# Experts of a two-layer kernel: first products from split weights, one token tile per group with weights at fixed addresses, further tiles by index

## What is computed

```python
N_GROUPS = 8; EXPERTS_PER_GROUP = 4; EXPERT_FF = 256; D_MODEL = 1024; SEQ = 512

def hierarchical_moe(h, w_router_group, b_router_group, w_router_expert, b_router_expert, w_gate, w_up, w_down):
    group_logits = jnp.matmul(h, w_router_group) + b_router_group
    g_sel = jnp.argmax(group_logits, axis=-1)
    ...
    combine = ...      # (512, 32): two non-zero weights in each token's row
    for e in range(32):
        hid = jax.nn.silu(jnp.matmul(h, w_gate[e])) * jnp.matmul(h, w_up[e])
        out = out + jnp.matmul(hid, w_down[e]) * combine[:, e:e + 1]
```

## Time and profile before

| | us |
|---|---|
| median of 3 runs | 3456.98 (3442.0 to 3465.07) |
| the profiled execution's own time | 3469.57 |
| its span, first to last instruction | 3467.7 |
| PE busy in the span | 3066.9 (88%) |
| DVE busy | 1723.3 (50%) |
| ACT busy | 1076.1 (31%) |
| mean DMA rate | 180 GB/s |

### The profile page before, as it was taken

One profiled execution on the slowest core, in us unless ns is written; L12 is line 12 of the kernel. 1 busy time (PEld: TensorE's weight loads), 2 busy tenths in 40 slices (PEclk: granted clock), 3 DMA queues, 4 the chain that ended last, 5 costly groups with the idle time before them and its releaser, 6 DMA issues. The chain is left out here.

```text
span 3467.7 us, 33649 instructions
## 1 busy us (share of the span) xinstructions
PE 3066.9 (88%) x12681; PEld 2229.5 (64%) x12681; DVE 1723.3 (50%) x3505; ACT 1076.1 (31%) x1596; POOL 488.8 (14%) x357
## 2 busy tenths in 40 slices
PE   7887999699999598778979879698898986999998
PEld 3445666444444244564746568698898986888887
DVE  2255422200000205543442328787879797788886
ACT  2133421100000126674421222234434443333332
POOL 0000000111111000000000000003314143344442
PEclk9995999699999798889779989899999998999999
DMA  3110061488888210021002211357859688999996
GB/s 142 44 50 25 1 145 64 194 329 309 313 315 309 85 49 37 25 97 44 1 26 102 83 55 61 123 193 246 324 178 336 233 305 292 342 369 374 368 374 238
DMA packets 159776, 624.04 MB, mean 180 GB/s; under 512 B 12161, under 2 KB 84481, under 8 KB 128257
## 3 DMA queue, kind: packets, MB, share of 16 engines
q1 hardware_dynamic: 90496, 319.87, 26.1%
q0 software_dynamic: 50688, 276.85, 21.1%
q10 hardware_dynamic: 18432, 25.17, 2.0%
HBM read 555.76 MB, written 66.09 MB: 179 GB/s over the span
## 5 line engine op out<-in xcount | busy, mean ns | idle before, releaser
L1841 POOL DMA_INDIRECT RG<-in_un,EI x128 | 181.6, 1419 | 1400.0 <-DVE EI L2060 1105.3
L2275 PE MATMUL bank<-VH,GL 128*128 128x512 f32 x768 | 300.2, 391 | 29.9 <-DVE VR0r L2264 29.9
L2277 PE MATMUL bank<-VH,GH 128*128 128x512 f32 x768 | 299.7, 390 | 0.0
L1841 POOL DMA_INDIRECT RG<-in_vn,EI x128 | 216.5, 1691 | 446.7 <-DVE X L1855 429.9
L1133 PE MATMUL bank<-UP,HX 128*128 128x512 f32 x480 | 213.0, 597 | 9.4 <-DVE HX L1087 5.5
L1194 DVE SCALAR_TENSOR_TENSOR HN<-SLU,HR,bank 128x256 f32<-128x256 f32 x44 | 21.1, 481 | 344.2 <-ACT SLU L1168 344.2
L2275 PEld LDWEIGHTS bank<-VH,GL 128*128 128x128 f32 x768 | 144.8, 189 | 60.7 <-issue 30.4
L1855 DVE SCALAR_TENSOR_TENSOR X<-RG,DG,X 128x1024 f32<-128x1024 f32 x128 | 164.1, 1282 | 28.2 <-DMA RG<-in_vn,EI 24.1
L1825 PE MATMUL bank<-HTl,UH1r 128*128 128x384 f32 x512 | 174.5, 341 | 0.0
L1826 PE MATMUL bank<-HTh,UH1r 128*128 128x384 f32 x512 | 174.2, 340 | 0.0
L1825 PE MATMUL bank<-HTl,UH0r 128*128 128x384 f32 x512 | 173.3, 338 | 0.0
(11 more groups left out here) (518 smaller groups left out, 6569.3 us busy)
## 6 DMA issues: line engine op xcount, KB each, us to landing
UR<-in_u SPq DMA_DIRECT2D x64, 1024.0 KB, 5.5
VR<-in_vn SPq DMA_DIRECT2D x32, 2048.0 KB, 9.2
W<-in_weights SPq DMA_DIRECT2D x20, 1536.0 KB, 7.3
W<-in_weights SPq DMA_DIRECT2D x14, 2048.0 KB, 8.2
aspill<-GA ACTq DMA_DIRECT2D x128, 192.0 KB, 2.0
wspill<-VR SPq DMA_DIRECT2D x12, 2048.0 KB, 9.2
WW<-wspill SPq DMA_DIRECT2D x32, 768.0 KB, 13.9
AV<-aspill SPq DMA_DIRECT2D x32, 768.0 KB, 16.0
```

The costliest lines, as they stand in the source:

```text
L1841: e.indirect_dma_start(RG[q % RR], None, d["un" if what == "u" else "vn"][:, :], off).then_inc(*row_in[q % RR].up(16))
L2275: e.matmul(bk, r(gl[:, a, t]), r(vh[:, a, :]), start=g == 0 and a == 0, stop=False)
L2277: i = e.matmul(bk, r(gh[:, a, t]), r(vh[:, a, :]), start=False, stop=g == 31 and a == 3)
```

## The change

- The gain goes into `XN` by DVE, 4 multiplies of 128 x 1024 with a row `GR` that SP loads, and no longer into `HX`.
- Slots: tile g (0 to 7) always belongs to group g. Only tokens past the 128th of a group go to tiles 8 to 10, which are given out by count. `IX` holds rows for these 12 units alone; for a tile that no group needs they lie past the end of the weights, and the gather is told to leave out such rows (`bounds_check`, `oob_is_err=False`).
- Units 0 to 31 have weights at fixed addresses. SP loads them: `UP` 0 and 1, and after the logits `DN` 0 to 2 and `UP` 2, in the routing block; the others in the experts block. POOL gathers those of units 32 to 43.
- `UP` is now `W2[n % 3][0]`, and `DN` has three buffers in place of four (two in HT's space).
- The first products become three fp32r passes. ACT makes `UPh` (2 copies of 128 x 2048 a unit) and DVE `UPl` (2 subtractions) one unit ahead, ACT makes `HXh` and DVE `HXl` for the tile. PE waits for each half of `UPl`.
- Weight tiles 21 to 23 are loaded at the end of SP's list in the experts block, and no longer in the routing block.

```diff
@@ routing block @@
-                        load_weights(e, 24)
+                        e.dma_start(GR, d["grow"][1]).then_inc(*gr_in.up(16))
+                        load_up(e, 0)
+                        load_up(e, 1)
+                        e.wait_ge(*e_logit(1))
+                        for n in range(3):
+                            load_dn(e, n)
+                        load_up(e, 2)
...
+                        e.wait_ge(*gr_in(16))
+                        for tb in range(4):
+                            e.tensor_tensor(XN[:, tb, 0:1024], XN[:, tb, 0:1024], GR, ALU.mult).then_inc(*e_gain.up(1))
...
-                        then(e.tensor_scalar(T9, T8, 128.0, None, ALU.mult))
-                        then(e.tensor_tensor(RK[:, 0:4, :], RK[:, 0:4, :], T9.unsqueeze(1).to_broadcast([128, 4, 8]), ALU.add))
+                        then(e.tensor_tensor(T8, T8, cc("iota")[:, 0:8], ALU.subtract))
+                        then(e.tensor_scalar(T9, T8, 128.0, 896.0, ALU.mult, ALU.add))
                         then(e.tensor_tensor(RK[:, 0:4, :], RK[:, 0:4, :], GO, ALU.mult))
-                        then(e.tensor_reduce(SF, RK[:, 0:4, :], AX.X, ALU.add))
+                        vs(e.tensor_reduce(SF, RK[:, 0:4, :], AX.X, ALU.add))
+                        then(e.tensor_tensor(S2, GO, bc(T9), ALU.mult))
+                        vs(e.tensor_reduce(MK, S2, AX.X, ALU.add))
+                        then(e.tensor_scalar(T8, cc("iota")[:, 0:8], 128.0, None, ALU.mult))
+                        then(e.tensor_tensor(S2, GO, bc(T8), ALU.mult))
+                        vs(e.tensor_reduce(s1[:, 0, :], S2, AX.X, ALU.add))
+                        then(e.tensor_scalar(s1[:, 1, :], SF, 127.5, None, ALU.is_gt))
+                        then(e.tensor_tensor(MK, MK, s1[:, 1, :], ALU.mult))
+                        then(e.tensor_tensor(SF, SF, s1[:, 0, :], ALU.add))
+                        then(e.tensor_tensor(SF, SF, MK, ALU.add))
@@ experts block @@
+            def act_tile(e, j, part):
+                e.wait_ge(*m_hturn(2 * j + part + 1))
...
+                e.activation(r(HXh[j % 2][:, span(part, 4), :]), bank[3].rearrange("p (a b) -> p a b", a=4), ACT.Copy).then_inc(*m_hxh.up(1))
+            def act_up(e, n):
+                wait_unit(e, n, up_in, up_in2)
+                if n >= 2:
+                    e.wait_ge(*m_up(n - 1))
+                for s in (span(0, 2048), span(1, 2048)):
+                    e.activation(r(UPh[n % 2][:, s]), UP[n % 3][:, s], ACT.Copy).then_inc(*m_uph.up(1))
+            def dve_up(e, n):
+                for q in range(2):
+                    s = span(q, 2048)
+                    e.wait_ge(*m_uph(2 * n + q + 1))
+                    e.tensor_tensor(r(UPl[n % 3][:, s]), UP[n % 3][:, s], UPh[n % 2][:, s], ALU.subtract).then_inc(*m_upl.up(1))
@@ POOL @@
-                    for n in range(NU):
...
+                    for n in range(4 * NG, NU):
+                        off = bass.IndirectOffsetOnAxis(ap=IX[:, n - 4 * NG:n - 4 * NG + 1], axis=0)
+                        e.wait_ge(*m_up(n - 2))
+                        e.indirect_dma_start(UP[n % 3], None, d["wup"][:, :], off, bounds_check=last, oob_is_err=False).then_inc(*up_in2[n % 3].up(16))
+                        e.wait_ge(*m_down(n - 2))
...
@@ SP @@
+                    for j in range(2):
+                        e.dma_start(HR[j], HS[span(j), :]).then_inc(*hr_in[j].up(16))
+                    for n in range(NU + 3):
+                        if 3 <= n < 4 * NG:
+                            e.wait_ge(*m_up(n - 2))
+                            load_up(e, n)
+                            e.wait_ge(*m_down(n - 2))
+                            load_dn(e, n)
+                        j, x = divmod(n, 4)
+                        if x == 0 and 2 <= j + 1 < NT and n:
+                            e.wait_ge(*m_hn(4 * j))
+                            e.dma_start(HR[(j + 1) % 2], HS[span(j + 1), :]).then_inc(*hr_in[(j + 1) % 2].up(16))
+                        if x == 2 and j >= 1:
+                            e.wait_ge(*m_outA(j))
+                            e.wait_ge(*m_outV(j))
+                            e.dma_start(OS[span(j - 1), :], OT[(j - 1) % 2]).then_inc(*os_done[(j - 1) % 2].up(16))
+                    load_weights(e, 24)
@@ PE @@
-                            for k in range(8):
-                                i = e.matmul(bank[n % 2], HX[j % 2][:, k, :], UP[n % 3][:, span(k, 512)], start=k == 0, stop=k == 7)
+                            for k in range(8):
+                                if k % 4 == 0:
+                                    e.wait_ge(*m_upl(2 * n + k // 4 + 1))
+                                s = span(k, 512)
+                                e.matmul(bank[n % 2], r(xl[:, k, :]), r(UPh[n % 2][:, s]), start=k == 0, stop=False)
+                                e.matmul(bank[n % 2], r(xh[:, k, :]), r(UPl[n % 3][:, s]), start=False, stop=False)
+                                i = e.matmul(bank[n % 2], r(xh[:, k, :]), r(UPh[n % 2][:, s]), start=False, stop=k == 7)
@@ ACT; DVE has dve_up and dve_tile at the same places @@
+                    act_up(e, 0)
+                    act_tile(e, 0, 0)
+                    act_tile(e, 0, 1)
                     for step in range(NU + 2):
                         n = step
+                        if n + 1 < NU:
+                            act_up(e, n + 1)
...
+                        j, x = divmod(step, 4)
+                        if x >= 2 and j + 1 < NT:
+                            act_tile(e, j + 1, x - 2)
```

More of the change, by code:

```diff
@@ L932, in program, with load_up, load_dn, wait_unit @@
             SL_ = sb("slot", [128, 4], c0, I32)
-            IX = sb("IX", [128, NU], c0, I32)
+            IX = sb("IX", [128, NU - 4 * NG], c0, I32)
             scattered = sem("scattered", True)
+            UP, UPl = [a for a, _ in W2], [a for _, a in W2]
+            DN = [HT.rearrange("p k n -> p (k n)")[:, span(n, 2048)] for n in range(2)] + [sb("DN2", [128, 2048], c0)]
+            up_in, dn_in = [sem(f"up_in{n}") for n in range(3)], [sem(f"dn_in{n}") for n in range(3)]
+            up_in2, dn_in2 = [sem(f"up_more{n}", True) for n in range(3)], [sem(f"dn_more{n}", True) for n in range(3)]
+            def load_up(e, n):
+                e.dma_start(UP[n % 3], d["wup"][span(n), :]).then_inc(*up_in[n % 3].up(16))
+            def load_dn(e, n):
+                e.dma_start(DN[n % 3], d["wdn"][span(n), :]).then_inc(*dn_in[n % 3].up(16))
+            def wait_unit(e, n, static, more):
+                if n < 4 * NG:
+                    e.wait_ge(*static[n % 3](16 * (n // 3) + 16))
+                else:
+                    before = len([m for m in range(4 * NG, n) if m % 3 == n % 3])
+                    e.wait_ge(*more[n % 3](16 * before + 16))
             with ExitStack() as c1:
@@ L1029, in _ @@
                         vs(e.tensor_reduce(XN[:, :, 1024:1028], oh.rearrange("p t (g x) -> p t x g", g=8), AX.X, ALU.add))
+                        bc = lambda a: a.unsqueeze(1).to_broadcast([128, 4, 8])
                         e.wait_ge(*e_count(1))
                         then(e.tensor_copy(RK, bank[1][:, 0:40].rearrange("p (b g) -> p b g", b=5)))
-                        then(e.tensor_scalar(TL, RK[:, 4, :], 0.0, None, ALU.is_gt))
-                        for j in range(1, 4):
+                        then(e.tensor_scalar(TL, RK[:, 4, :], 128.0, None, ALU.is_gt))
+                        for j in range(2, 4):
                             then(e.tensor_scalar(T8, RK[:, 4, :], 128.0 * j, None, ALU.is_gt))
@@ L1047, in _ @@
                         then(e.tensor_reduce(GI, GT, AX.X, ALU.add))
-                        then(e.tensor_scalar(GI, GI, 7.0, 512.0, ALU.min, ALU.mult))
-                        then(e.tensor_tensor(IF, cc("rows").unsqueeze(1).to_broadcast([128, NT, 4]), col(GI).to_broadcast([128, NT, 4]), ALU.add))
+                        then(e.tensor_scalar(GI, GI, 512.0, None, ALU.mult))
+                        then(e.tensor_tensor(IF, cc("rows").unsqueeze(1).to_broadcast([128, 3, 4]), col(GI).to_broadcast([128, 3, 4]), ALU.add))
@@ L1057, in _ @@
                             e.indirect_dma_start(HS[:, :], bass.IndirectOffsetOnAxis(ap=SL_[:, tb:tb + 1], axis=0), XN[:, tb, :], None).then_inc(*scattered.up(16))
-            UP = [sb(f"UP{n}", [128, 4096], c0) for n in range(2)] + [HT.rearrange("p k n -> p (k n)")]
-            DN = [sb(f"DN{n}", [128, 2048], c0) for n in range(4)]
+            UPh = [sb(f"UPh{n}", [128, 4096], c0) for n in range(2)]
             HR = [sb(f"HR{n}", [128, 1028], c0) for n in range(2)]
-            HX = [sb(f"HX{n}", [128, 8, 128], c0) for n in range(2)]
+            HXh, HXl = ([sb(f"{x}{n}", [128, 8, 128], c0) for n in range(2)] for x in ("HXh", "HXl"))
             SLU, HN = ([sb(f"{x}{n}", [128, 256], c0) for n in range(2)] for x in ("SLU", "HN"))
@@ L1065, in program @@
             OT = [sb(f"OT{n}", [128, 1024], c0) for n in range(2)]
[L1066 to L1068 removed]
```

(15 more changed lines are left out.)

43 lines of the change are left out of this document (16 added, 27 removed).

## The result

The changed kernel takes 3541.55 us (median of 4 runs, 3534.76 to 3558.93) beside 3461.03 before (median of 4 as well); the ratio is 1.0238, interval 1.0166 to 1.031: slower, 10.5 us over the forecast and inside its range. The profiled execution took 3539.16, its span is 3537.4, 69.7 more than before.

A forecast was written before the change was run, and what follows sets the result against it. PE bounds the stage before; after the change, late-issued UP loads and their landing would. Stage 47, clock 20, start 2 and end 5 sum to +74 on 3469.57: 3543.6, or 3531 as median; range 3483 to 3578.

The forecast's parts named there:

- The step of PE, 9.24 us: Experts stage: PE's work per unit falls from 10.52 to 9.24 us with three fp32r passes, 1.28 less.
- A tile before, 43.0: Experts stage of the kernel before: four steps of 10.52 us plus the tile's own transposes, 43.0 us.
- When SP asks for weights: SP's list in experts: UP n+1 stands behind DN n's wait, leaving one step (9.24 us) of lead; 14.0 needed, plus 0.3.
- The four steps, 51.8 us a tile: Experts, tiles with SP-loaded weights: steps of 11.3, 13.8, 10.1 and 16.6 us, 51.8 a tile, 8.8 more than before.
- Steps 32 to 45, -16: End of experts, where SP loads no weights: left-out gathers cost near nothing, 9.24 a step and 1.6 a tile, -16 us.
- Rival 3: Gathers in experts: rows left out cost as much as rows moved, +40 us over the forecast, 3571; chance 0.08.
- Clock, +20: Experts: PE's eight rests of 7 us lower its clock, 2.5 us each, +20 in all, bounds 0 and +35.
- Start: Routing and first unit: multiplies by GR hidden, slot chain +1.4 us, first unit and tile halves about +0.5.
- Tail, +5: End of experts: loads of weight tiles 21 to 23 meet the gather of rows, which takes twice its 5 us, +5.
- 1: Experts: PE stays the bound and loads are hidden, -42 us, 3415; chance 0.04.
- 2: Experts: landing is the limit, but mildly, within 1%: about +36 us, 3493, or 3483; chance 0.11.
- 4: Experts: the clock stays down through the stage, +150 us over the forecast, 3680; chance 0.03.

The follow-up runs named there:

- tail alone: Changed kernel with SP waiting for the gathers of result rows before loading weight tiles 21 to 23: 3544.3 us, ratio 1.0252 to before.
- order and tail: Changed kernel with each UP and POOL gather asked for once its buffer is free, weight tiles 21 to 23 loaded after the result-row gather: 3404.6 us, 0.9838 to before.

## Why the prediction was right, step by step

- *The step of PE, 9.24 us:* right, 9.2 in the kernels with early loads. *A tile before, 43.0:* 44.0 between `HH` copies. The first step of a tile is 12.0, with 0.8 us in which PE waits for `HX`, and that wait was not in the 43.0; the 473.3 us that seemed to agree end before the last steps' second products.
- *When SP asks for weights:* right, and the one that carries the result. The order alone is worth 119 us of S.
- *The four steps, 51.8 us a tile:* 55.1 measured with the clock's part, forecast 54.3 (51.8 + 2.5). By the means of tiles 2 to 7 the x = 2 step was 0.7 shorter, x = 1 and x = 3 longer by 1.6 and 2.4, where the low clock falls.
- *Steps 32 to 45, -16:* mis-sized. I took a left-out gather at near nothing. It moves nothing, but it has an issue of 1 to 3 us on POOL and 2.1 to landing, with 4.3 of splits behind, and two of them follow the end of a step. The tiles took 42.3, and 39.2 without the gathers: about 9 us more than forecast. Rival 3 (40 more) did not come.
- *Clock, +20:* about 15, by the scaled estimate above. I had counted eight rests of 7 us; the rests at x = 1 lowered the clock too, so there were 17 falls. At x = 3 a step takes 1.9 to 2.7 us more than its rest and 9.6, close to the 2.5 that I took. At x = 1 the slow products take as much again (1.8 to 2.7), and yet the total is not twice as large: that they lie in time without weights anyway is my reading, which no run tests alone.
- *Start:* the multiplies by `GR` were hidden (4.62 us, and DVE still waited 5.6 for the logits). From the logits to the slots it took 12.2 us where it was 11.15: +1.1, forecast +1.4. R fell by 2.2 all the same, with the clock at 0.60 in it and not 0.55; in the three runs with the same routing that reached it at 623 us, as before did, R was 50.5 to 51.0 and not 47.4, so the fall belongs to the execution.
- *Tail, +5:* mis-sized, +10, and 12 for the gather itself (tail alone). I had read the 4.7 us of `HR` loads beside weights as evidence that small rows suffer little, and that reading was wrong: they did not meet. In the profile of before, while the `HR` load issued at 937.4 moved its rows (939.6 to 941.6), the queue of the weights moved 0.03 MB; at the end 6.3 MB stood in line. The packets of 1232 to 1244 in the changed kernel, the loads' queue and the gathers':

```profile
q1 hardware_dynamic: 282, 4.15, 80.7%
q0 software_dynamic: 279, 1.02, 20.8%
```

As many packets of each (of 4096 bytes in the gathers' queue and of 16384 in the loads', apart from some 30 of 4 bytes in each), so four times the bytes for the loads. The turn-taking packet by packet that the Trainium skill states ("DMA: Bandwidth & Descriptors", Queues, rings and completion order) would have given +10. The trace agrees: equal counts, and 16.9 us to landing with the three loads ahead, 5.3 without.
- The stage's sum was +67.5 and is +73.0; with the tail 5 over, R and the start 4 under, and 3 behind that nothing explains, the total was 74 beside 69.7 + 14.2 = 84 for the profiled execution without what it gained ahead of the change, and 80.5 between the medians. The mechanism is right, but part of the closeness is luck: the terms that were too small (gathers 9, tail 5) and too large (clock 5, R) partly cancel.
- *Rivals.* 1 (loads hidden, 3415) is what the kernel does once the order is changed: 3430.5. Its condition was read rightly, `UP` did not go out early. 2 and 4 did not come: the clock recovered after each rest.

## What to carry to other kernels

A list of loads in program order has a lead that is set by its latest wait: before taking a buffer away, find which load stands behind that buffer's wait, and count from the issue, not from the buffer's own release. Order the list by when each wait ends; here that was worth 3% of the kernel, 119 us of S, where the cheaper products give 4.6 us a tile, some 50. A split inserted between landing and use takes its time from the same lead, and puts every later entry of that engine's list (`HN`, `HXl`, the copy that frees a store) behind the transfer as well.

## What the runs showed of the hardware that I had not expected

A gather by index with all rows left out moves none of its 1 or 2 MB (0.01 MB in the gathers' queue from 1100 to 1150 us, with ten such gathers), and still takes POOL 0.99 to 3.0 us and 2.1 to 4.1 us to land: too long where a step waits for it, free where each is asked for as soon as its own buffer is free (39.2 us a tile in "order and tail", as with no gather at all). Gathers of 4 KB rows that met 6.3 MB of plain loads landed after 16.9 us in place of 5.3, with packets of the two queues moving one for one.
